# Layer norm's scaling on GpSimd and attention's probabilities turned by VectorE and transfers, in a trunk that TensorE bounds

## What is computed

```python
x = layer_norm(ALPHA * x + 0.5 * swiglu(x, ffn1...), ln1_g[l], ln1_b[l])
mix = hybrid_mixer(x, w_in[l], ...)       # ONE projection, three token mixers
x = layer_norm(ALPHA * x + mix, ln2_g[l], ln2_b[l])
x = layer_norm(ALPHA * x + 0.5 * swiglu(x, ffn2...), ln3_g[l], ln3_b[l])
```

## Time and profile before

| | us |
|---|---|
| median of the 3 runs (lowest, highest) | 1097.84 (1097.4, 1098.56) |
| the profiled execution, its own time | 1098.82 |
| its span in the profile | 1097.0 |
| TensorE busy | 1080.1 |
| VectorE busy | 766.2 |
| ScalarE busy | 580.0 |
| GpSimd busy | 134.7 |

### The profile page before, as it was taken

How to read it: one execution, slowest core, us unless ns; L and a number is a source line. 1 busy time by engine, 2 the same in 40 slices (tenths; PEclk the granted TensorE clock), 3 DMA queues, 4 the chain that set the end, 5 groups by cost and what they waited for, 6 DMA issues and landing times.

```text
span 1097.0 us, 14535 instructions
## 1 busy us (share of the span) xinstructions
PE 1080.1 (98%) x5329; PEld 896.1 (82%) x5329; DVE 766.2 (70%) x764; ACT 580.0 (53%) x647; POOL 134.7 (12%) x137
## 2 busy tenths in 40 slices
PE   9799999999999999999999999999999999999997
PEld 6688888899888788888878888879988887888885
DVE  5556556789979775555678665577999786755556
ACT  5555555569454544444456655556774536444441
POOL 1298000000000000000005980000000000000000
PEclk9899999999999999999999999999999999999999
DMA  8776778455555477677757767774455673777770
GB/s 248 241 250 226 220 229 249 125 183 167 169 174 183 164 264 248 215 233 233 245 147 247 258 219 229 259 202 143 158 171 154 192 254 130 242 239 231 234 239 38
DMA packets 192368, 226.37 MB, mean 206 GB/s; under 512 B 31540, under 2 KB 157128, under 8 KB 192328
## 3 DMA queue, kind: packets, MB, share of 16 engines
q1 hardware_dynamic: 192328, 225.83, 65.1%
HBM read 214.26 MB, written 11.53 MB: 206 GB/s over the span
## 4 chain that ended last, share of the span: by engine, by line
PE 95%; SPq 2%; DMA 1%; issue 1%; DVE 1%; ACT 0%; POOLq 0%; DVEq 0%; POOL 0%
PE ps L561 26%; PE ps L538 18%; PE ps L540 18%; PE ps L539 18%; PE ps L522 2%; PE ps L523 2%; PE ps L524 2%; PE ps L907 1%; PE ps L906 1%; PE ps L905 1%; PE ps L574 1%; PE ps L835 1%; SPq L442 1%; PE ps L822 0%; DMA raw<-in_ffn_w_up 0%
## 5 line engine op out<-in xcount | busy, mean ns | idle before, releaser
L1370 DVE TENSOR_TENSOR w_lo<-raw,w_hi 128x2048 fp32r<-128x2048 f32 x173 | 400.2, 2316 | 184.9 <-ACT w_hi L989 184.2
L989 ACT CAST w_hi<-raw 128x2048 fp32r<-128x2048 f32 x173 | 330.1, 1910 | 194.6 <-PE ps L561 86.5
L538 PE MATMUL ps<-w_hi,xT 128*128 128x512 f32 x848 | 331.7, 391 | 0.5 <-DVE w_lo L1382 0.2
L540 PE MATMUL ps<-w_hi,xT 128*128 128x512 f32 x848 | 330.2, 389 | 0.0
L539 PE MATMUL ps<-w_lo,xT 128*128 128x512 f32 x848 | 330.1, 389 | 0.0
L538 PEld LDWEIGHTS ps<-w_hi,xT 128*128 128x128 f32 x848 | 159.2, 188 | 36.5 <-issue 3.6
L540 PEld LDWEIGHTS ps<-w_hi,xT 128*128 128x128 f32 x848 | 159.2, 188 | 33.3
L539 PEld LDWEIGHTS ps<-w_lo,xT 128*128 128x128 f32 x848 | 159.3, 188 | 32.6
L561 PE MATMUL ps<-w_hi,rows_hi 128*128 128x512 f32 x416 | 134.8, 396 | 5.7 <-DVE rows_lo L1413 5.7
L561 PE MATMUL ps<-w_hi,rows_lo 128*128 128x512 f32 x416 | 133.1, 392 | 0.0
L561 PE MATMUL ps<-w_lo,rows_hi 128*128 128x512 f32 x416 | 133.0, 392 | 0.0
(11 more groups left out here) (227 smaller groups left out, 1138.7 us busy)
## 6 DMA issues: line engine op xcount, KB each, us to landing
raw<-in_ffn_w_down SPq DMA_DIRECT2D x44, 1024.0 KB, 5.3
raw<-in_ffn_w_gate SPq DMA_DIRECT2D x86, 512.0 KB, 4.0
raw<-in_ffn_w_up SPq DMA_DIRECT2D x86, 512.0 KB, 5.1
raw<-in_w_in SPq DMA_DIRECT2D x30, 1024.0 KB, 5.2
hid_dram<-qT SPq DMA_DIRECT2D x160, 64.0 KB, 2.3
qT<-hid_dram SPq DMA_DIRECT2D x40, 256.0 KB, 2.7
raw<-in_w_out SPq DMA_DIRECT2D x8, 1024.0 KB, 4.9
raw<-in_w_in SPq DMA_DIRECT2D x8, 512.0 KB, 4.8
```

Source lines behind the costliest of these rows:

```text
L538: mm(o, xT[:, c, 0, tok], h, start=c == UPPER_FIRST[0], stop=False, skip_group_check=True)
L540: return mm(o, xT[:, c, 1, tok], h, start=False, stop=c == UPPER_FIRST[-1], skip_group_check=True)
L989: nc.scalar.copy(w_hi[s][:, :], raw[s][:, :]).then_inc(hi_made.sem, 1)
L1370: tt(w_lo[s][:, :], raw[s][:, :], f32(w_hi[s][:, :]), ALU.subtract).then_inc(lo_made.sem, 1)
```

## The change

1. `params` is called behind the third turn of SyncE's loop (after the steps 2 to 4) instead of ahead of the loop.
2. `scaled_back(l, 0)` is taken from VectorE; GpSimd does the same two operations, as soon as the tile's transposes are made. ScalarE waits for it ahead of `gate(1, 0)`, VectorE ahead of the block transposes and the next norm.
3. TensorE's 24 transposes of the probabilities and ScalarE's six copies are gone. VectorE turns 32x32 blocks of `S1` behind `scan(1)` and of `S0` behind `turn_out(1)` (`probs_blocks`), SyncE stores them to DRAM in four transfers each and reads each back in one (1 MB and 0.5 MB each way, a layer).
4. TensorE does `gates_lower(1)` right behind `gates_upper(1)`, and `attend(1)` behind `gates_lower(2)`; ScalarE's and VectorE's work on its result (`attn_hi`, `attn_rest`) moves with it, `attn_rest(1, 1)` from before `scan(2)` to before `scan(3)`.

```diff
@@ SyncE
+            def probs_out(l, blk):
+                src = blocks_second if blk else blocks_first
+                sp.wait_ge(pblocks_made.sem, pblocks_made.at(l, 2 - blk))
+                for a in range(4):
+                    sp.dma_start(probs_dram[blk].rearrange("g i a r -> a i g r")[a],
+                                 src[32 * a:32 * a + 32, :].rearrange("i (g r) -> i g r", g=4)
+                                 ).then_inc(pblocks_out[blk].sem, 16)
+            def probs_back(l, blk):
+                sp.wait_ge(pblocks_out[blk].sem, pblocks_out[blk].at(l, 1))
+                sp.dma_start(turned_second if blk else turned_first,
+                             probs_dram[blk].rearrange("g i a r -> (g i) (a r)")).then_inc(probs_turned[blk].sem, 16)
...
-                after_step()
-                with sp.Fori(2, STEPS) as i:
...
+                with sp.Fori(2, 5) as i:
+                    step(i)
+                after_steps()
+                with sp.Fori(5, STEPS) as i:
+                    step(i)
...
+                    if p == 3:
+                        probs_out(l, 0)
+                        probs_back(l, 1)
+                        probs_back(l, 0)
+                        load(l, MIX0 + PAIR0 + 2 * p + 1, gate_pair(l, p, 0))
+                    else:
+                        load(l, MIX0 + PAIR0 + 2 * p + 1, gate_pair(l, p, 0))
+                    if p == 2:
+                        probs_out(l, 1)
@@ TensorE
-                        pe.wait_ge(pT_made.sem, pT_made.at(l, 4))
...
-                    pe.wait_ge(pT_made.sem, pT_made.at(l, 4 if blk else 6))
-                    held = probsT if blk else probsT_first
+                    pe.wait_ge(probs_turned[blk].sem, probs_turned[blk].at(l, 1))
+                    held = (turned_second if blk else turned_first).rearrange("p (a k j) -> p k a j", a=4, j=32)
...
-                transpose_probs(S1, 4, 0)
-                transpose_probs(S0, 2, 4)
                 gates_upper(1)
+                gates_lower(1)
                 output_states(0)
                 input_states(1)
-                attend(1)
-                gates_lower(1)
                 gates_upper(2)
                 gates_lower(2)
+                attend(1)
@@ ScalarE
-                sc_.wait_ge(x_made.sem, x_made.at(l, 2))
                 read(BB, cv_b[:, :, :])
...
-                probs_out(0, 4)
-                probs_out(4, 2)
                 split(l, MIX0 + 13)
+                sc_.wait_ge(x_made.sem, x_made.at(l, 2))
+                gate(1, 0)
+                gate(1, 1)
                 states(2)
-                attn_hi(1, 1)
                 split(l, MIX0 + 14)
                 states(3)
-                gate(1, 0)
-                gate(1, 1)
                 split(l, MIX0 + 15)
                 split(l, MIX0 + 16)
+                sc_.wait_ge(pblocks_out[1].sem, pblocks_out[1].at(l, 1))
                 gate(2, 0)
                 gate(2, 1)
+                attn_hi(1, 1)
@@ GpSimd
                 deviations(l, 0)
+                pool.wait_ge(gb_landed.sem, gb_landed.at(l, 2))
+                pool.wait_ge(tp_made.sem, tp_made.at(l, NT))
+                gain, shift = (gb[:, n, :].rearrange("p (o d) -> p o d", o=1).to_broadcast([P, NT, D]) for n in (0, 1))
+                tt(xtok[:, :, :], xtok[:, :, :], gain, ALU.mult).then_inc(pool_chain, 1)
+                pool.wait_ge(pool_chain, links.next())
+                tt(xtok[:, :, :], xtok[:, :, :], shift, ALU.add).then_inc(x_made.sem, 1)
@@ VectorE
+                def probs_blocks(S, out, blk):
+                    dve.wait_ge(probs_made.sem, probs_made.at(l, 2 - blk))
+                    if blk:
+                        dve.wait_ge(x_made.sem, x_made.at(l, 2))
+                    nc.vector.transpose(out.rearrange("p (g k j) -> p g k j", g=4, j=32),
+                                        S[:, :, :].rearrange("p h (b g j) -> p g (h b) j", g=4, j=32)
+                                        ).then_inc(pblocks_made.sem, 1)
...
                 lo(3)
-                scaled_back(l, 0)
...
                 scan(1)
+                probs_blocks(S1, blocks_second, 1)
                 lo(12)
                 turn_out(1)
+                probs_blocks(S0, blocks_first, 0)
                 lo(13)
...
                 lo(14)
-                attn_rest(1, 1)
                 scan(2)
...
                 lo(17)
+                attn_rest(1, 1)
                 scan(3)
...
+                dve.wait_ge(x_made.sem, x_made.at(l, 2))
                 norm(l, 1, FFN0[1] - 1, 1.0, lambda lower: None)
```

More of the change, by code:

```diff
@@ L128, in trunk @@
             [("xTf", [P, KC, SEQ], F32), ("gb", [P, 2, D], F32)])
-        probsT_first = gates[:, 5, :, :].rearrange("p t (h n) -> p (t h) n", n=P)
+        turned_first = gates[:, 5, :, :].rearrange("p t n -> p (t n)")
         probsT, rows_hi, rows_lo = overlay(
@@ L133, in trunk @@
             [("rows_hi", [P, 2, 2, SEQ], F32R), ("rows_lo", [P, 2, 2, SEQ], F32R)])
+        turned_second = probsT[:, :, :].rearrange("p h n -> p (h n)")
+        blocks_second = gates[:, 3:5, :, :].rearrange("p b t n -> p (b t n)")
         S1, y_attn = overlay([("S1", [P, HEADS, 2 * P], F32)], [("y_attn", [P, 4, 2, SEQ], F32R)])
+        blocks_first = S1[:, 0:4, :].rearrange("p h n -> p (h n)")
         b_in = S1[:, 0, :].rearrange("p (r t c) -> p r t c", r=2, t=STATE_TILES)
@@ L194, in trunk @@
         ps = ctx.enter_context(nc.psum_tensor("ps", [P, 8, 512], F32))
+        probs_dram = [nc.dram_tensor(f"probs_dram{n}", (4, 32, 4, n * HEADS * 32), F32, kind="Internal").ap()
+                      for n in (1, 2)]
         hid_dram = nc.dram_tensor("hid_dram", (4, 32, 4, P), F32, kind="Internal").ap()
@@ L263, in trunk @@
         probs_made = Events(sem("probs_made"), 2)
-        pT_done = Events(sem("pT_done"), 6)
-        pT_made = Events(sem("pT_made"), 6)
+        pblocks_made = Events(sem("pblocks_made"), 2)
+        pblocks_out = [Events(sem(f"pblocks_out{n}"), 1, unit=64) for n in range(2)]
+        probs_turned = [Events(sem(f"probs_turned{n}"), 1, unit=16) for n in range(2)]
         pv_done = Events(sem("pv_done"), 2)
@@ L364, in turn_hidden, with load_ffn @@
                 sp.dma_start(hid_turned, hid_dram.rearrange("g i a r -> (g i) (a r)")).then_inc(h_turned.sem, 16)
-            def load_ffn(l, f, w_gate, w_up, w_down, after_two, after_step, before_last):
+            def probs_out(l, blk):
[9 more added lines that the diff above has]
+                             probs_dram[blk].rearrange("g i a r -> (g i) (a r)")).then_inc(probs_turned[blk].sem, 16)
+            def load_ffn(l, f, w_gate, w_up, w_down, after_two, after_steps, before_last):
                 k0 = FFN0[f]
@@ L382, in load_ffn, with step @@
                 load(l, k0 + 4, rows(w_down, l, 0))
-                after_step()
-                with sp.Fori(2, STEPS) as i:
+                def step(i):
                     load(l, k0 + i * 3 - 1, gate_up(w_gate, w_up, l, 1, i * 256), 2)
@@ L474, in _ @@
                     load(l, MIX0 + PAIR0 + 2 * p, gate_pair(l, p, 1))
-                    load(l, MIX0 + PAIR0 + 2 * p + 1, gate_pair(l, p, 0))
+                    if p == 3:
[7 more added lines that the diff above has]
+                        probs_out(l, 1)
                     if p == 3:
@@ L868, in _ @@
                 gates_lower(0)
-                pe.wait_ge(bu_made.sem, bu_made.at(l, 2))
-                pe.wait_ge(probs_made.sem, probs_made.at(l, 1))
-                transpose_probs(S1, 4, 0)
-                pe.wait_ge(probs_made.sem, probs_made.at(l, 2))
-                transpose_probs(S0, 2, 4)
                 gates_upper(1)
-                pe.wait_ge(pT_made.sem, pT_made.at(l, 6))
+                gates_lower(1)
                 output_states(0)
                 input_states(1)
-                attend(1)
-                gates_lower(1)
                 gates_upper(2)
                 gates_lower(2)
+                attend(1)
                 gates_upper(3)
@@ L1162, in normalise @@
                     last.then_inc(probs_made.sem, 1)
[L1164 to L1170, removed]
                 def attn_hi(n, blk):
                     sc_.wait_ge(pv_done.sem, pv_done.at(l, n))
+                    if blk:
+                        sc_.wait_ge(pblocks_out[0].sem, pblocks_out[0].at(l, 1))
                     nc.scalar.copy(y_attn[:, :, 0, blk * P:blk * P + P], ps[:, 3, :].rearrange("p (m q) -> p m q", m=4)
```

## The result

The changed kernel takes 1111.47 us (median of 4 runs, 1110.29 to 1114.12) against 1098.12 us: ratio 1.0124, 95% interval 1.0111 to 1.0136. It is 13.4 us slower, where 6.9 were forecast, and lies 1.5 us above the range. The direction, the places and the lengths of the instructions came out as worked out; two terms did not.

The account below looks back on a forecast made before the run. TensorE, busy 98% of the span, was taken to bound the kernel. 1097.0 - 8.3 (opening) + 13.4 (scaling) + 1.8 (probabilities) = 1103.9 us of span, 1104.7 us on the median; range 1091.5 to 1110 us.

Parts of the forecast that it names:

- Scaling on GpSimd: Behind each first norm: GpSimd instructions of 4.66 us hold VectorE's `xT`, TensorE waits; 6.7 us a layer, 13.4 us lost.
- Rival 1: At `xT` in both layers: GpSimd's long instruction does not hold VectorE throughout; 1091.3 to 1095.3 us, chance 0.25.
- so I put no clock loss into the sum: At the scaling: idle times of 3.2 and 3.55 us, shorter than before the opening's fall, were given no clock cost.
- Rival 2: The clock falls too, at the scaling or the mixer's wait, 2.8 us each; 1107.5 to 1116 us, chance 0.22.
- Opening: Parameters' transfers out of the way, the first hidden block is stored at 22.0 us, not 27.15; 8.3 us gained, once.
- Probabilities: In the mixer: 2.62 us of TensorE transposes a layer go, VectorE gets 3.40 us; 0.9 us a layer longer, 1.8 both.
- the first gates: In the mixer: without the transposes as cover, TensorE waits for ScalarE's reading of the first gate; 0.33 us paid back.
- chunk 14: In the middle of the gates: its `w_lo` ends at 290.21 us, wanted at 287.16; TensorE waits some 3 us.
- transfers of 3 MB a layer cost nothing: In the mixer: the probabilities' stores and returns were costed at nothing, unless they took more than 13 us.
- rival 4: At the scaling: a cheap GpSimd instruction of 3.0 to 3.8 us; 1097 to 1101 us, chance 0.06.

Follow-up runs that it names:

- e9: The changed kernel with TensorE's waits filled by products nobody reads (11, 9 and 10); 1108.92 us, ratio 1.0094 to the kernel before.
- e1: The changed kernel with the residual scaling back on VectorE; 1096.2 us, ratio 0.9981 to the kernel before.
- e4: The kernel before with only the residual scaling moved to GpSimd; 1113.38 us, ratio 1.0139.
- e5: The kernel before with only the scaling on GpSimd, in eight instructions of 128x512 instead of two of 128x2048; 1102.55 us, ratio 1.0035.
- e3: The kernel before with only the mixer edit (attention's probabilities turned by VectorE and transfers); 1104.19 us, ratio 1.0049.
- e6: The mixer edit alone on the kernel before, with 11 unread products filling TensorE's wait for chunk 14; 1100.77 us, ratio 1.0019.
- e2: The kernel before with only the parameters' transfers moved behind the third turn of SyncE's loop; 1092.06 us, ratio 0.9945.
- e8: The kernel before with the parameters' transfers spread over the first three turns of SyncE's loop; 1091.8 us, ratio 0.9940.
- e11: The mixer edit alone on the kernel before, with the convolution's scaling and additions left out on VectorE; 1098.75 us, ratio 1.0003.
- e10: The kernel before with only the scaling on GpSimd, started behind the second tile's last `xT`; 1106.03 us, ratio 1.0071.

## Why the prediction came out as it did

- **Scaling on GpSimd: mechanism and waits right.** 4.54 and 4.62 us for 4.66; a stretch 6.4 us a layer longer with the clock kept (e9) for 6.7; e1 and e4 show that it is this edit (15.3 and 14.9 us), e5 that the instruction's length is what counts. Rival 1 (the hold given up early) is out.
- **The step that failed: "so I put no clock loss into the sum".** It read one fall, after over 4 us of idle time, as if shorter idle times were safe. e3's fall followed 2.44 us of idle time. e6 shows a share of 3.4 us for the mixer alone, e9 one of 2.6 us for the whole change. Rival 2 was what happened: in the profiled execution a fall in the scaling's stretch in layer 0 (1.1 us), one in layer 1 (2.7 us) and one in the mixer in layer 1 (1.5 us), by the stretches against e9's. A fall is not sure: in layer 0 of the same execution the mixer's wait was as long, 2.45 us, and the clock stayed. Nor does every fall cost: e4's in layer 0 did not.
- **Opening: mechanism right, the term too large.** 8.3 us were forecast, 6.4 measured (e2). The store left at 21.9 us as worked out, but the block came back late: TensorE still waited 0.9 us. At the new place the transfers took 9.4 us of the queue and not 7.5 or less, and in the changed kernel one later step waited 0.4 us more. That the place as such costs the rest is not shown: e8 spread them and gained nothing. The profiled execution of e2, its fastest, is 7.6 us shorter than that of the kernel before, which with its wait of 0.8 us is nearly the forecast; why the medians are only 6.4 us apart stays open.
- **Probabilities: right in size.** 0.9 us a layer were forecast, 1.0 is there with the clock kept (e6, e9). The single terms: block transposes of 2.29 and 1.24 us, 0.42 us at the first gates for 0.33, and 2.45 us for chunk 14 for 3.2. These waits less the 2.62 us of transposes make only 0.25 us. The rest is in the first product behind each stop or change of work, which takes 0.43 to 0.47 us in the chain where the others take 0.23; e6 has three such places more than the kernel before, some 0.7 us in all. What the forecast did not see is the dependence behind the wait (e11): with a lighter VectorE it would have been wrong. That transfers of 3 MB a layer cost nothing fits e11, where the waits left (1.6 and 0.42 us) and those first products account for its stretch; no run leaves the transfers out.
- **The sum.** 13.4 - 6.9 = 6.5 us were missing. The clock makes 2.6 of them (e9), the opening 1.9 and the mixer 0.3, while the scaling's waits came out 0.5 us shorter. That leaves about 2.2 us. In the profiled executions of the changed kernel and of e9, 1.1 and 1.2 us of it lie between VectorE's last instruction and the end of the span (3.6 us for 2.4), which no other run has, and 0.4 us more than before between the first mixer's gated linear unit and the next layer's transposes. The cause of both stays open, as does the rest.
- **Small slips.** By the prediction's own formula, rival 4 would give 1098 to 1101 us, and the change would break even at 2.9 us and not 3.0. Nothing hangs on either.

The best version is the first edit alone: e2 (1092.06 us) or e8 (1091.8 us), 0.6% faster than the kernel before and 1.8% faster than the changed one.

## What to carry to other kernels

Before work is moved to GpSimd, look which two-input instructions of VectorE run beside it and who waits for them; a long GpSimd instruction held each of them to its own end here, and splitting it shortened the single holding more than the sum of them (e5: 5.5 us for 7.4). When work leaves the engine that bounds the kernel, follow the queue of the engine that takes it to the next thing that the bound waits for: here 2.6 us of TensorE's work were exchanged for 3.5 us on a VectorE with nothing to spare. Count a wait of TensorE with the low clock that may follow it, and not alone: here waits of 1.6 us left the clock up (e5, e11), and behind or in most of those of 2.3 to 3.0 us it fell.

## What the runs showed of the hardware

The clock can fall after the wait is over: in e3's layer 0 TensorE was idle for 2.44 us, ran 0.8 us at 2.4 GHz, and then 1.2 GHz was granted for about 3.4 us (290.7 to 294.1), with TensorE busy throughout. In e10's layer 1 it fell 1.3 us behind a wait of 2.28 us, in e4's layer 0 still inside the wait of 2.77 us. In the changed kernel's layer 1 the clock stayed low for 10 us over a second wait. Products whose results nobody reads, put into the wait, kept it at 2.4 GHz and made the kernel faster by 3.4 us (e6). GpSimd's instruction, for its part, takes 6.52 instead of 4.6 us where VectorE is first (e10).
